# Output projection of a hybrid layer: seven block products for eight, with the block sums made during earlier stages

## The reference, cut to what matters

```python
proj = x @ w_in[l]                       # then split among the branches
y_a, y_b, y_c, y_m = (... @ p_a[l]), (... @ p_b[l]), (... @ p_c[l]), (... @ p_m[l])
gates = jax.nn.sigmoid(g.reshape(bsz, seq, N_BRANCH, D_MODEL))
merged = (gates[:, :, 0] * y_a + gates[:, :, 1] * y_b
          + gates[:, :, 2] * y_c + gates[:, :, 3] * y_m)
out = merged @ w_out[l]
x = _layer_norm(ALPHA * x + out, ln_g[l], ln_b[l])
```

## Time and profile before

| | |
|---|---|
| median of 3 runs | 1223.14 us (1223.01 to 1223.56) |
| profiled execution: its time, its span | 1223.87 us, 1222.1 us |
| PE busy in the span | 1203.0 us, 98% |
| DVE, ACT, POOL busy | 781.5, 539.5, 693.5 us |
| granted PE clock, mean | 0.999 of full |

### The profile page before, as it was taken

One profiled execution on the slowest core, in us unless ns is written; L12 is line 12 of the kernel. 1 busy time (PEld: TensorE's weight loads), 2 busy tenths in 40 slices (PEclk: granted clock), 3 DMA queues, 4 the chain that ended last, 5 costly groups with the idle time before them and its releaser, 6 DMA issues.

```text
span 1222.1 us, 15758 instructions
## 1 busy us (share of the span) xinstructions
PE 1203.0 (98%) x5704; PEld 999.2 (82%) x5704; DVE 781.5 (64%) x1285; ACT 539.5 (44%) x992; POOL 693.5 (57%) x550
## 2 busy tenths in 40 slices
PE   7999999999999999999999999999999999999997
PEld 6888888888888888888888888888888888878886
DVE  4723765677566674438587665666666786876755
ACT  5433434344443443557354565656556444315000
POOL 5677887887777777777226444455533225547000
PEclk9999999999999999999999999999999999999999
DMA  8022131232323423234412111111002533376131
GB/s 278 1 69 69 35 104 35 69 138 101 106 105 103 138 104 104 104 105 148 162 53 56 32 53 52 35 53 46 24 18 92 191 111 116 105 260 241 66 130 69
DMA packets 91277, 118.61 MB, mean 97 GB/s; under 512 B 6072, under 2 KB 72632, under 8 KB 91200
## 3 DMA queue, kind: packets, MB, share of 16 engines
q1 hardware_dynamic: 91200, 117.60, 29.2%
HBM read 92.39 MB, written 25.20 MB: 96 GB/s over the span
## 4 chain that ended last, share of the span: by engine, by line
PE 86%; DVE 7%; ACT 3%; issue 2%; DMA 1%; POOL 1%; DVEq 0%; SPq 0%; ACTq 0%
PE pj L745 11%; PE pj L746 11%; PE pj L747 11%; PE pj L816 5%; PE pj L817 5%; PE pj L818 5%; PE pj L1074 4%; PE pt L746 3%; PE pt L747 3%; PE pt L745 3%; PE po L930 3%; PE pt L917 2%; PE po L1074 2%; PE pt L1074 2%; PE pj L833 2%
## 5 line engine op out<-in xcount | busy, mean ns | idle before, releaser
L1571 POOL TENSOR_TENSOR ring_lo<-w_pair,ring_hi 128x512 fp32r<-128x512 f32 x168 | 232.3, 1385 | 111.3 <-ACT ring_hi L1130 111.1
L1624 POOL TENSOR_TENSOR w_lo<-w_raw,w_hi 128x128 fp32r<-128x128 f32 (+1 forms) x104 | 111.2, 1088 | 161.6 <-ACT w_hi L1220 159.5
L1130 ACT ACTIVATE ring_hi<-w_pair 128x512 fp32r<-128x512 f32 x168 | 105.1, 628 | 160.6 <-PE pj L747 108.6
L1785 DVE SCALAR_TENSOR_TENSOR po<-glu,cwa,po 128x512 f32<-128x512 f32 x232 | 159.4, 747 | 20.6 <-ACT po L1181 20.6
L745 PE MATMUL pj<-t_hi,ring_hi 128*128 128x512 f32 x392 | 152.8, 390 | 0.3 <-DVE slot L1749 0.3
L746 PE MATMUL pj<-t_lo,ring_hi 128*128 128x512 f32 x392 | 152.5, 389 | 0.0
L747 PE MATMUL pj<-t_hi,ring_lo 128*128 128x512 f32 x392 | 152.5, 389 | 0.0
L816 PE MATMUL pj<-xT_hi,w_hi 128*128 128x512 f32 x320 | 126.5, 395 | 0.0
L817 PE MATMUL pj<-xT_lo,w_hi 128*128 128x512 f32 x320 | 125.4, 392 | 0.0
L818 PE MATMUL pj<-xT_hi,w_lo 128*128 128x512 f32 x320 | 125.0, 391 | 0.0
L1664 POOL TENSOR_SCALAR probs<-probs,rinv 128x128 f32<-128x128 f32 (+3 forms) x32 | 57.9, 1810 | 110.8 <-DVE rinv L2103 110.8
(11 more groups left out here) (344 smaller groups left out, 2952.1 us busy)
## 6 DMA issues: line engine op xcount, KB each, us to landing
w_pair<-in_w_in SPq DMA_DIRECT2D x28, 1024.0 KB, 5.2
gate_scratch<-slot SPq DMA_DIRECT2D x16, 1024.0 KB, 4.0
gate<-gate_scratch SPq DMA_DIRECT2D x32, 512.0 KB, 3.8
w_raw<-in_w_in SPq DMA_DIRECT2D x20, 512.0 KB, 3.9
z_scratch<-slot SPq DMA_DIRECT2D x8, 512.0 KB, 2.6
bias<-cum_scratch SPq DMA_DIRECT2D x8, 512.0 KB, 3.8
wout_raw<-in_w_out SPq DMA_DIRECT2D x8, 512.0 KB, 5.5
x_tok<-in_x SPq DMA_DIRECT2D x8, 512.0 KB, 4.3
```

Source lines behind the costliest of these rows:

```text
L1130: nc.scalar.activation(ring_hi[:, j % RING, :, :], w_src(u, p), ACT.Copy).then_inc(s_rhi, 1)
L1571: nc.gpsimd.tensor_tensor(ring_lo[:, j % RING, :, :], w_src(u, p), ring_hi[:, j % RING, :, :], ALU.subtract).then_inc(s_rlo, 1)
L1624: nc.gpsimd.tensor_tensor(w_lo[:, j % 2, k, :], w_raw[:, j % 2, k, :], w_hi[:, j % 2, k, :], ALU.subtract).then_inc(s_wlo, 1)
L1785: nc.vector.scalar_tensor_tensor(out=acc if n < PAD_A else src, in0=src, scalar=cwa[:, ct, n:n + 1], in1=acc, op0=ALU.mult, op1=ALU.add).t ...
```

## The change

The output projection is made for two token tiles (256 tokens, `u` = 0 to 3) at a time by seven products (`p` in the order 1, 5, 6, 2, 7, 3, 4) of a 128x512 block of `merged` by a 512x512 block of `w_out` or of a sum of such blocks. Each product is 4 blocks of the contraction by 3 products of the split: 12 matmuls, and 4 x 7 x 12 = 336 in all.

What this takes, beside the products:

- `w_out` is loaded as four blocks of 512x512 (1 MB each): 11 and 12 at M3 and M4, 22 at M6, 21 at C3. Four sums of blocks are made (`block_sum`), each one instruction over 128x2048 elements: numbers 1 and 3 on POOL, behind `split_w` of M6 and of M7, numbers 2 and 4 on DVE, behind C2 and C3. The seven blocks are split: hi on ACT (beside C3 to C7 and after), lo on DVE (`out_block_lo` 0 to 6, each 128x2048, reading raw and hi) beside C3 to C7 and after.
- For each `u` POOL makes four sums of 128x512 of `merged` (`merged_sum`) and seven lo parts of 128x512 (`out_lo`), ACT seven hi parts into a ring of five and three copies of banks (`out_copy`). PE waits for each lo part.
- DVE adds the residual to the three copies (`with_copy`, reading two SBUF tiles), then the bank to that (`out_result`); the normalisation of a tile keeps its two passes.
- The last two C tiles run by token halves: C6 and C7 for tokens 0 to 511, then C6 and C7 for 512 to 1023. DVE, not POOL, adds these four halves to `merged`.
- The gates of M2 to M5 are loaded together at M1, into another place; x and the layer norm's parameters are loaded once P_C is done.

```diff
+    OU = NT // 2
+    OSEQ = [(u, p) for u in range(OU) for p in ORDER]
+    NOQ = len(OSEQ)
+    OSLOT = {up: j for j, up in enumerate(OSEQ)}
+    O_RING = 5
+    OUT_B = {1: 0, 5: 1, 6: 2, 2: 3, 7: 4, 3: 5, 4: 6}
+    LAST_C = S_END - 2
+
+
+    def half_no(s, h):
+        return 2 * s + h + 1 if s < LAST_C else 2 * LAST_C + 2 * h + s - LAST_C + 1
...
+    ob11, ob_t1, ob_t2, ob21, ob_t3, ob22, ob_t4 = ob_raw
+    ob12 = ob_t3
...
+                if s == S_OF[BR_M, 1]:
+                    for dt in range(2, 6):
+                        load_gate(S_OF[BR_M, dt])
...
+                if s == S_OF[BR_M, 3]:
...
+                    load_out_block("11", ob11, 0, 0)
+                if s == S_OF[BR_M, 4]:
+                    load_out_block("12", ob12, 0, 1)
+                if s == S_OF[BR_M, 6]:
+                    load_out_block("22", ob22, 1, 1)
+                if s == S_OF[BR_C, 3]:
+                    sp.wait_ge(s_addm, ADDM_NO[S_OF[BR_M, 5]])
+                    load_out_block("21", ob21, 1, 0)
+
+            sp.wait_ge(s_pj, 2 * S_END)
...
+            for h in range(2):
+                for s in range(LAST_C, S_END):
+                    pe.wait_ge(s_pjfree, 2 * s + h - 3)
+                    p_steps(s, h, 0, CT, 2 * ((s + 1) % 2) + h)
...
+                pe.wait_ge(s_orl, j + 1)
+                if u == 0:
+                    pe.wait_ge(s_obl, OUT_B[p] + 1)
+                dst = out_bank(u, p)
+                for k in range(KH):
+                    w_h, w_l = o_ring_hi[j % O_RING][:, k, :], o_ring_lo[j % O_RING][:, k, :]
+                    hi, lo = ob_hi[OUT_B[p]][:, k, :], ob_lo[OUT_B[p]][:, k, :]
+                    nc.tensor.matmul(dst, w_h, hi, start=k == 0 and p in (1, 2, 5), stop=False, skip_group_check=True)
+                    nc.tensor.matmul(dst, w_h, lo, start=False, stop=False, skip_group_check=True)
+                    mm = nc.tensor.matmul(dst, w_l, hi, start=False, stop=k == KH - 1, skip_group_check=True)
+                mm.then_inc(s_out_pj, 1)
...
+            for s in range(S_P + IN_M + 2, S_END):
+                split_w(s // 2, s % 2, p_k(s))
+                if s >= S_END - 5:
+                    out_block_hi(s - (S_END - 5))
+            out_block_hi(5)
+            for j in range(3):
+                out_ring_hi(j)
+            out_block_hi(6)
+            for j in range(3, O_RING):
+                out_ring_hi(j)
+            for u in range(OU):
+                for p in ORDER:
+                    if u and p == 1:
+                        out_std(2 * u - 1)
+                    if p in (1, 5, 6):
+                        out_copy(u, p)
+                    if OSLOT[u, p] + O_RING < NOQ:
+                        out_ring_hi(OSLOT[u, p] + O_RING)
+                    if p == 4:
+                        out_std(2 * u)
+            out_std(NT - 1)
...
+            def block_sum(n):
+                if n == 1:
+                    pool.wait_ge(s_wo["11"], 16)
+                    pool.wait_ge(s_wo["12"], 16)
+                    dst, in0, in1 = ob_t1, ob12, ob11
+                else:
+                    pool.wait_ge(s_wo["22"], 16)
+                    pool.wait_ge(s_ot, 1)
+                    dst, in0, in1 = ob_t3, ob22, ob12
+                nc.gpsimd.tensor_tensor(dst[:, :, :], in0[:, :, :], in1[:, :, :], ALU.subtract).then_inc(s_ot, 1)
...
+                if s == S_OF[BR_M, 6]:
+                    block_sum(1)
+                if s == S_OF[BR_M, 7]:
+                    block_sum(3)
...
+                nc.gpsimd.tensor_tensor(o_ring_lo[j % O_RING][:, :, :], out_src(*OSEQ[j]), o_ring_hi[j % O_RING][:, :, :],
+                                        ALU.subtract).then_inc(s_orl, 1)
...
+                nc.gpsimd.tensor_tensor(dst, in0, in1, op).then_inc(s_osum, 1)
+
+            for u in range(OU):
+                for p in ORDER:
+                    if p == 1 and u:
+                        merged_sum(u, 1)
+                        merged_sum(u, 3)
+                    out_lo(OSLOT[u, p])
+                    if p == 1:
+                        if u == 0:
+                            merged_sum(u, 1)
+                            merged_sum(u, 3)
+                        merged_sum(u, 2)
+                    if p == 2:
+                        merged_sum(u, 4)
...
+                if s >= LAST_C:
+                    dve.wait_ge(s_pjfree, half_no(s, h))
+                    dve.wait_ge(s_addm, ADDM_NO[S_OF[BR_M, dt]])
+                    nc.vector.tensor_tensor(merged[:, dt, hs(h)], merged[:, dt, hs(h)], gate, ALU.add).then_inc(s_addc, 1)
...
+            def block_sum(n):
+                if n == 2:
+                    dve.wait_ge(s_ot, 2)
+                    dst, in0, in1 = ob_t2, ob22, ob_t1
+                else:
+                    dve.wait_ge(s_ot, 3)
+                    dve.wait_ge(s_wo["21"], 16)
+                    dst, in0, in1 = ob_t4, ob21, ob_t2
+                nc.vector.tensor_tensor(dst[:, :, :], in0[:, :, :], in1[:, :, :], ALU.subtract).then_inc(s_ot, 1)
+
+            def out_block_lo(n):
+                dve.wait_ge(s_obh, n + 1)
+                nc.vector.scalar_tensor_tensor(out=ob_lo[n][:, :, :], in0=ob_raw[n][:, :, :], scalar=0.5,
+                                               in1=ob_hi[n][:, :, :], op0=ALU.mult, op1=ALU.subtract).then_inc(s_obl, 1)
...
+            for s in range(S_P + IN_M, LAST_C):
                 for h in range(2):
                     p_half(s, h, 2 * ((s + 1) % 2) + h)
+                if s == S_OF[BR_C, 2]:
+                    block_sum(2)
+                if s == S_OF[BR_C, 3]:
+                    block_sum(4)
+                    out_block_lo(0)
+                if s == S_OF[BR_C, 4]:
+                    out_block_lo(1)
+                if s == S_OF[BR_C, 5]:
+                    out_block_lo(2)
+            for h in range(2):
+                for s in range(LAST_C, S_END):
+                    p_half(s, h, 2 * ((s + 1) % 2) + h)
+                    if h == 0:
+                        out_block_lo(3 + s - LAST_C)
+            for n in (5, 6):
+                out_block_lo(n)
...
+                v = x_tok[:, q, hs(h)]
+                nc.vector.scalar_tensor_tensor(out=v, in0=v, scalar=ALPHA, in1=o_cp[p][:, :], op0=ALU.mult,
+                                               op1=ALU.add).then_inc(s_pre, 1)
...
+            for u in range(OU):
+                for p in (1, 5, 6):
+                    with_copy(u, p)
+                for p in (2, 7, 3):
+                    out_result(u, p)
+                out_mean(2 * u)
+                if u < OU - 1:
+                    out_norm(2 * u)
+                    out_result(u, 4)
+                    out_mean(2 * u + 1)
+                    out_norm(2 * u + 1)
+            out_norm(NT - 2)
+            out_result(OU - 1, 4)
+            out_mean(NT - 1)
+            out_norm(NT - 1)
```

More of the change, by code:

```diff
@@ L690, in first_rows, with out_bank, out_src @@
                     w_pair[u][:, k, :].rearrange("p (n c) -> p n c", n=2))
+        def out_bank(u, p):
+            return bank((4 + 3 * u + {1: 0, 6: 0, 7: 0, 4: 0, 2: 1, 5: 2, 3: 2}[p]) % 8)
+        def out_src(u, p):
+            if p == 5:
+                return o_s1[:, :, :]
+            k0, n = {1: (0, 0), 6: (0, 0), 2: (KH, 0), 3: (KH, 0), 7: (0, 1), 4: (KH, 1)}[p]
+            return merged[:, k0:k0 + KH, (2 * u + n) * P:(2 * u + n + 1) * P]
+        O_SUM_NO = {(u, n): 4 * u + i + 1 for u in range(OU) for i, n in enumerate((1, 3, 2, 4))}
         @block.tensor
@@ L1053, in _ @@
                     mscores(w + 2)
-            for s in range(S_P + IN_M, S_END):
+            for s in range(S_P + IN_M, LAST_C):
                 for h in range(2):
@@ L1064, in _ @@
                         mweigh(NT - 1)
-            def out_bank(n):
-                return bank((n + 4) % 8)
-            def out_step(n, k, part):
-                tk, c = slice(n // 2 * P, (n // 2 + 1) * P), slice(n % 2 * HALF, (n % 2 + 1) * HALF)
-                m_hi, o_hi = merged_hi[:, k, tk], wout_hi[k][:, c]
-                m, o = ((m_hi, o_hi), (m_hi, wout_lo[k][:, c]), (merged_lo[:, k, tk], o_hi))[part]
-                mm = nc.tensor.matmul(out_bank(n), m, o, start=k == 0 and part == 0, stop=k == KT - 1 and part == 2)
-                if k == KT - 1 and part == 2:
-                    mm.then_inc(s_out_pj, 1)
@@ L1102, in w_src @@
+            for j in range(NOQ):
+                out_product(j)
         def w_src(u, p):
@@ L1552, in _, with out_block_hi @@
-            for s in range(S_P + IN_M + 2, S_END):
-                split_w(s // 2, s % 2, p_k(s))
-                if s >= S_END - 4:
-                    merged_hi_make(s - (S_END - 4))
-                    wout_hi_make(s - (S_END - 4))
-            for k in range(4, KT):
-                wout_hi_make(k)
-                merged_hi_make(k)
-            for t in range(NT):
+            def out_block_hi(n):
+                if n == OUT_B[1]:
+                    act.wait_ge(s_ot, 1)
```

(38 more changed lines are left out.)

211 lines of the change are left out of this document (109 added, 102 removed).

## The result

The changed kernel takes 1237.37 us (median of 4 runs, 1235.98 to 1239.22) against 1223.35 (1223.01 to 1223.66) for the kernel before on the same chip: ratio 1.0115, 95% interval 1.0103 to 1.0127, so 14 us slower. Predicted were 1243.8 with a range from 1234 to 1250. The profiled execution has a span of 1235.9, 13.8 above that of before.

The account below looks back on a forecast made before the run. PE, busy 98% of the span, was taken as the bound: 1222.1 - 10.9 (48 fewer matmuls) + 8.0 + 6.6 + 8.7 + 0.9 + 5.1 + 1.3 + 1.0 = 1242.8, as a median 1243.8; range 1234 to 1250.

Parts of the forecast that it names:

- The queue of DVE and POOL: Instructions of the two engines that read two SBUF tiles exclude each other for their whole length and take turns.
- The two rivals without exclusion: No exclusion that counts: 1220.7, chance 0.05; only tensor_tensor held, scalar_tensor_tensor not: 1225.5, chance 0.07.
- M tiles, +8.0: POOL's block sums 1 and 3, 4.75 us each, hold DVE's adds; C2 begins at 1102.6 instead of 1094.6.
- The third rival: DVE idles while POOL sums, PE catches up, M tiles cost +0 to +2: 1236 to 1238, chance 0.1.
- C tiles, +6.6: Sums 2, 4 and lo parts on DVE share the queue with POOL; P_C ends at 1141.9 instead of 1135.3.
- Wait ahead of product 1, +8.7, and product 2, +0.9: Output start: an 18.9 us queue delays product 1's lo part to 1153.3; lo 6 and another delay product 2.
- Clock, +1.0: PE's idleness ahead of product 1 lowers the clock; its 12 matmuls may cost 2.7 us, in part hidden.
- fourth rival: Statistics join the queue, or the clock falls in the M tiles too: 1248 to 1251, chance 0.12.
- The pairs, +5.1: Output stage: the queue needs 20.7 us a pair against PE's 19.04, 1.7 for each of three pairs.
- a sign of being wrong: Output pairs: the prediction would be wrong if PE kept 19.04 us a pair.
- Statistics at nothing: Output stage: statistics read one SBUF tile and are taken as outside the queue, 0; the bound is 7 us.
- Tail, +1.3: After PE's last matmul DVE finishes tile 6 before tile 7's last half: +1.8, less 0.5 for the first pass.

Follow-up runs that it names:

- no_pool_sums: Changed kernel with block sums 1 and 3 on POOL cut to 2 of 512 columns each, waits and loads kept: 1230.8 us, ratio 1.0062.
- both runs with pieces: Changed kernel, four 128x512 instructions each: POOL's block sums 1 and 3 (1239.02 us, ratio 1.0127); DVE's sums 2 and 4 and block lo parts (1247.9, 1.0199).
- root_early: Changed kernel plus a one-column square root on ACT ahead of the loop over the C tiles: 1237.44 us, ratio 1.0113.
- sums_adds_on_dve: Changed kernel with block sums 1 and 3 and the adds of C2 to C5, by halves, moved from POOL to DVE: 1234.86 us, ratio 1.0087.

## Why the prediction held, and which steps didn't

- **The queue of DVE and POOL.** Held: the adds of 4.36 and 4.34, gone with the sums (no_pool_sums). The two rivals without exclusion, 1220.7 and 1225.5, are out, the second by low parts, each a scalar_tensor_tensor, stretched from 2.28 to 4.25 as well. That the turn is per instruction is shown by both runs with pieces.
- **M tiles, +8.0.** The mechanism was right, the size was 6.4. A sum takes 5.06, my upper estimate, not 4.75. But sum 1 began at 1088.46 and not 1087.7, and the add that it held asked 1.25 us into it; so PE had one bank more ahead of each sum than in my order. The third rival is out too: DVE did not idle beside the sums, and the M tiles cost 6.4 and not 0 to 2. That the measured time lies within its 1236 to 1238 is chance.
- **C tiles, +6.6.** 39.4 against 32.8: 6.6. The two queues run in the order on record, instruction by instruction, 21.6 us long (1109.95 to 1131.59) where I had 22.8. But from w_lo of C7 to the end of P_C it is 8.8 us and not 7.5, since PE ran C7's first 7 matmuls at the lower clock, 3.1 us for 1.6. Two errors of 1.2 and 1.3 cancelled; the exact 6.6 is luck.
- **Wait ahead of product 1, +8.7, and product 2, +0.9.** 5.96 and 0. Here too every instruction on record was in the chain. From the add of C5 (1131.55) to the lo part of product 1 (1149.07) it is 17.5 us, where I had 18.9, and it began 2.9 earlier, while PE ended P_C only 1.5 earlier: 8.7 - 1.4 - 2.9 + 1.5 = 5.9. Each turn taken whole, as I did, makes the queue too long. Product 2's low part was hidden by product 1 at the lower clock.
- **Clock, +1.0.** 2.5: all 12 matmuls of product 1 ran at the lower level. I had taken most of it as hidden behind POOL. By the trace only 0.5 was: POOL had product 2's low part ready at 1152.35, and at the full clock product 1 would have ended at 1151.84. Half of the fourth rival's condition came true, and without its 3 to 5 us: the clock fell in the M tiles (0.50 from 1097 to 1099) and M7's 12 matmuls took 4.2 us instead of 2.7, but C2 waited another 2.08 for its bank anyway. In C7 (0.50 from 1131 to 1133) it is held in the +6.6. The granted clock of the row that I had sized the term on the earlier trace rows reads 1.00; what bears the term out is product 1 itself, a matmul every 0.43 us at 0.50.
- **The pairs, +5.1.** This step failed: 0. PE kept its 19.04 us (a pair takes 19.27), which the prediction itself had named as a sign of being wrong. I had added up whole instructions, 14.1 + 6.6 = 20.7, against PE's 19.04. By the trace a `with_copy` of 0.61 puts a POOL instruction off by 0.35 to 0.45 (1.74 for 1.29), the one pass that meets a single POOL instruction by 0.8 (2.09 for 1.29), and a pass can fall in part where POOL is idle; the seven add 4.4 and not 6.6, and 18.5 is less than 19.04. In the C tiles the queue was 1.2 shorter than my sum and in the chain to product 1 1.4; that these have the same cause is likely, but no run separates it.
- **Statistics at nothing.** Right: 0.69 beside POOL's instructions, as without them. The Trainium skill (SBUF — State Buffer, Who interferes with whom) says so of a DVE instruction with one SBUF input, and the trace agrees.
- **Not on record at all:** the table load in the chain of tile 0; the pause at product 9 is 1.65 in this trace, and root_early takes 1.1 of it away and shows nothing in the median.
- **Tail, +1.3.** 1.4.

The errors are -1.6, 0, -2.7, -0.9, +1.5, -5.1, +1.65 and +0.1, with 0.3 of small pauses: -6.8, from 1242.8 to 1236.0, and the trace has 1235.9. Without the failed step the forecast would have been 1238.7. What stays open is why seven products for eight can't be brought to pay here: the experiments show each wait taking another's place between 1100 and 1165, on DVE, POOL and ACT in turn, but not that an order without them is impossible.

## What to carry to other kernels

Saving one matmul in eight of a stage on an engine that is 98% busy paid here only as far as its helpers had room in the very 60 us in which the new sums fall; and two engines that read two SBUF tiles per instruction must be added up as one. Move shared work to the engine on which it is shorter (2.28 on DVE against 5.06 on POOL for the same sum; with the adds, this won 3 us in sums_adds_on_dve), keep it in whole instructions where that engine is the late one, and count less than its full length for each turn in the queue. A pause of PE costs more than itself where the clock falls: 6.0 us without work became 8.5.
